# Block scores of the chunked linear attention: seven masks per (head, 128-frame tile) with one multiply and one sum, in place of seven predicated copies per head

## The reference

```
S_t = diag(exp(log_g_t)) S_{t-1} + k_t v_t^T,    o_t = S_t^T q_t
```

## The kernel before

| slot | tile | steps, before |
|---|---|---|
| 18, 20, 21, 22 | f, g, q, v | (2,0)(2,1) / (2,2)(2,3) / (3,0)(3,1) / (3,2)(3,3) |
| 31, 32, 33 | q, v, g | (5,1) / (5,2)(5,3) / (6,0) |
| 35, 36, 37 | g, g, g | (6,1) / (6,2) / (6,3) |
| 38, 39, 40 | none | (7,0) / (7,1) / (7,2)(7,3) |

## Time and profile before

### The profile page before, as it was taken

The page is one execution under the profiler, slowest core; times in us unless marked ns, Lnnn a source line. Parts: engine busy times, 40 slices in busy tenths (PEclk is TensorE's granted clock), DMA queues, the critical chain, the costliest instruction groups (busy, mean ns, idle before and its releaser), DMA issues.

```text
span 1369.5 us, 15843 instructions
## 1 busy us (share of the span) xinstructions
PE 1283.1 (94%) x5841; PEld 1017.8 (74%) x5841; DVE 687.8 (50%) x933; ACT 480.3 (35%) x754; POOL 250.0 (18%) x201
## 2 busy tenths in 40 slices
PE   5899999888889999999997999999799999999996
PEld 3678787676668888888885686656668888888884
DVE  7556767663475343343435555563474343343434
ACT  4444454343233232232433453232333242332322
POOL 2321212201188300000004700000281000000012
PEclk8999999899999999999999999999999999999997
DMA  3321121113214333333332322101223333333321
GB/s 111 108 62 53 41 61 49 46 48 108 77 46 116 93 93 106 94 92 99 95 99 62 77 74 50 46 16 45 78 62 97 100 97 93 97 102 92 92 77 62
DMA packets 212607, 106.62 MB, mean 78 GB/s; under 512 B 20385, under 2 KB 210946, under 8 KB 212546
## 3 DMA queue, kind: packets, MB, share of 16 engines
q1 hardware_dynamic: 211938, 103.42, 26.5%
q0 software_dynamic: 608, 2.36, 0.5%
HBM read 103.67 MB, written 2.10 MB: 77 GB/s over the span
## 4 chain that ended last, share of the span: by engine, by line
PE 84%; DVE 8%; ACT 4%; DMA 2%; issue 1%; POOL 1%; POOLq 0%; ACTq 0%; DVEq 0%; SPq 0%
PE bank L1257 24%; PE bank L1259 24%; PE bank L1258 24%; DVE y L918 2%; PE pp L1372 2%; PE pp L1524 2%; PE pp L1523 2%; PE po L1541 1%; PE pp L1369 1%; DVE h_lo L925 1%; DMA x_tok<-in_x 1%; POOL xT L551 1%; ACT w_hi L403 1%; DVE w_lo L410 1%; PE misc L1303 0%
## 5 line engine op out<-in xcount | busy, mean ns | idle before, releaser
L1257 PE MATMUL bank<-h_lo,w_hi 128*128 128x512 f32 (+1 forms) x848 | 343.9, 406 | 36.7 <-DVE h_lo L925 25.2
L403 ACT CAST w_hi<-stage 128x1024 fp32r<-128x1024 f32 (+2 forms) x192 | 199.1, 1037 | 410.6 <-DMA stage<-in_mlp_w 308.7
L1258 PE MATMUL bank<-h_hi,w_lo 128*128 128x512 f32 (+1 forms) x848 | 335.4, 396 | 0.0
L1259 PE MATMUL bank<-h_hi,w_hi 128*128 128x512 f32 (+1 forms) x848 | 334.7, 395 | 0.0
L410 DVE TENSOR_TENSOR w_lo<-stage,w_hi 128x1024 fp32r<-128x1024 f32 (+2 forms) x192 | 241.6, 1259 | 65.5 <-PE bank L1259 57.2
L1257 PE MATMUL bank<-a_lo,w_hi 128*128 128x512 f32 x656 | 257.1, 392 | 2.2 <-DVE y L1094 2.2
L1258 PE MATMUL bank<-a_hi,w_lo 128*128 128x512 f32 x656 | 255.9, 390 | 0.0
L1259 PE MATMUL bank<-a_hi,w_hi 128*128 128x512 f32 x656 | 255.8, 390 | 0.0
L1257 PEld LDWEIGHTS bank<-h_lo,w_hi 128*128 128x128 f32 (+1 forms) x848 | 161.7, 191 | 86.6 <-issue 41.2
L1258 PEld LDWEIGHTS bank<-h_hi,w_lo 128*128 128x128 f32 (+1 forms) x848 | 161.8, 191 | 35.2 <-issue 2.2
L1259 PEld LDWEIGHTS bank<-h_hi,w_hi 128*128 128x128 f32 (+1 forms) x848 | 161.3, 190 | 35.9 <-issue 0.6
(11 more groups left out here) (244 smaller groups left out, 1149.5 us busy)
## 6 DMA issues: line engine op xcount, KB each, us to landing
stage<-in_mlp_w SPq DMA_DIRECT2D x128, 512.0 KB, 4.1
stage<-in_ev_w_in SPq DMA_DIRECT2D x28, 512.0 KB, 3.7
stage<-in_ev_w_out SPq DMA_DIRECT2D x8, 512.0 KB, 4.1
stage<-in_od_w_out SPq DMA_DIRECT2D x8, 512.0 KB, 4.1
stage<-in_od_w_in SPq DMA_DIRECT2D x5, 512.0 KB, 3.9
x_tok<-in_x SPq DMA_DIRECT2D x4, 512.0 KB, 5.5
x_tok<-in_x POOLq DMA_DIRECT2D x1, 2048.0 KB, 8.4
stage<-in_mla_w_ukv SPq DMA_DIRECT2D x8, 256.0 KB, 3.0
```

The lines of the kernel that those rows point to most:

```text
L403: nc.scalar.copy(w_hi[:, u % SPLIT, 0:n], stage[:, u % STAGE, 0:n]).then_inc(hi_ready, 1)
L1257: nc.tensor.matmul(dst, wh, xl_, start=first, stop=False)
L1258: nc.tensor.matmul(dst, wl, xh, start=False, stop=False)
L1259: return nc.tensor.matmul(dst, wh, xh, start=False, stop=last)
```

## The change

A step becomes one (head, tile) instead of one or two planes for all tiles. PE makes the seven planes of one tile, nine matmuls, into pp0 or pp1 (two of them go round, by p_read). DVE multiplies the 896 columns by the seven masks into tmp and sums the seven planes by a `tensor_reduce` whose innermost axis steps by 128 elements (512 bytes) into one of four 128x128 buffers. Plane 0's mask is now all ones: the parts of plane 0 that no matmul writes are zeroed once at the start (two memsets of 128x128 for one of 128x512). The outputs of a tile follow two long slots behind its own step. The assignment of steps to slots is the same, four per head.

```diff
-            pending = [pending[1], [(o, c) for o, step in groups if step == len(STEPS) - 1 for c in range(NT)]]
+            pending = [pending[1], groups]
@@ pool
-            for r, c in ((slice(0, 64), slice(64, 128)), (slice(0, 32), slice(32, 64)), (slice(64, 96), slice(96, 128))):
-                ch.link(nc.gpsimd.memset(masks[r, 0, c], 1.0))
+            ch.link(nc.gpsimd.memset(masks[:, 0, :], 1.0))
@@ vector
-            nc.vector.memset(pp[0][:, 0:4, :], 0.0).then_inc(p_zero, 1)
+            for b in range(2):
+                nc.vector.memset(pp[b][:, 0, :], 0.0).then_inc(p_zero, 1)
@@
-            def group(o, step):
-                a = a_bufs[o % 2]
-                if step == 0 and o < 2:
-                    nc.vector.memset(a, 0.0).then_inc(a_zero, 1)
-                    dve.wait_ge(a_zero, o + 1)
-                elif step == 0:
-                    dve.wait_ge(o_done, o - 1)
-                for plane in STEPS[step]:
-                    n = o * PAIRS + plane
-                    dve.wait_ge(p_done, n + 1)
-                    if plane:
-                        dve.wait_ge(a_ready, n)
-                    mask = masks[:, plane:plane + 1, :].to_broadcast([P, NT, P])
-                    nc.vector.copy_predicated(a, mask.bitcast(I32), planes[n % 4]).then_inc(a_ready, 1)
-                if step == 2 and FIRST[PACK_OF[o]] == o:
+            def group(o, c):
+                idx = o * NT + c
+                pm = tmp[:, :, :].rearrange("p a t -> p (a t)")[:, 0:PAIRS * P]
+                dve.wait_ge(p_done, idx + 1)
+                if idx >= 1:
+                    dve.wait_ge(a_ready, idx)
+                nc.vector.tensor_tensor(pm, pp[idx % 2][:, 0:PAIRS, :].rearrange("p l t -> p (l t)"),
+                                        masks[:, :, :].rearrange("p l t -> p (l t)"), ALU.mult).then_inc(p_read, 1)
+                dve.wait_ge(p_read, idx + 1)
+                nc.vector.tensor_reduce(a_sb[:, idx % 4, :], pm.rearrange("p (l t) -> p t l", l=PAIRS),
+                                        AX_X, ALU.add).then_inc(a_ready, 1)
+                if c == 2 and FIRST[PACK_OF[o]] == o:
                     update_state(PACK_OF[o])
@@ tensor
-            def pairs(o, step):
...
+            def pairs(o, c):
+                p, idx, r, s = PACK_OF[o], o * NT + c, head_rows(o), slice(c * P, (c + 1) * P)
+                pe.wait_ge(xl_ready, (p + 1) * (LEVELS + 2))
+                if idx >= 2:
+                    pe.wait_ge(p_read, idx - 1)
+                else:
+                    pe.wait_ge(p_zero, idx + 1)
+                for lv in range(2):
+                    L = 64 >> lv
+                    for b in range(0, P, 2 * L):
+                        nc.tensor.matmul(pp[idx % 2][b:b + L, 0, b + L:b + 2 * L], xls[p % 2][r, lv, c * P + b:c * P + b + L],
+                                         xls[p % 2][r, lv, c * P + b + L:c * P + b + 2 * L], start=True, stop=True)
+                for lv in range(2, LEVELS):
+                    nc.tensor.matmul(pp[idx % 2][:, lv - 1, :], xls[p % 2][r, lv, s], xls[p % 2][r, lv, s],
+                                     start=True, stop=True)
+                nc.tensor.matmul(pp[idx % 2][:, PAIRS - 1, :], ks[p % 3][r, s], qs[p % 3][r, s], start=True,
+                                 stop=True).then_inc(p_done, 1)
@@ outputs
-                pe.wait_ge(a_ready, (o + 1) * PAIRS)
-                ins = nc.tensor.matmul(po[:, s], vbuf[:, o % 4, s], a_bufs[o % 2][:, c, :], start=True, stop=(c == 0))
+                pe.wait_ge(a_ready, idx + 1)
+                ins = nc.tensor.matmul(po[:, s], vbuf[:, o % 4, s], a_sb[:, idx % 4, :], start=True, stop=(c == 0))
```

More of the change, by code:

```diff
@@ L46 @@
 PAIRS = 7
-STEPS = [(0, 1), (2, 3), (4, 5), (6,)]
 Q_RANK_T, KV_RANK_T = 3, 2
@@ L297, in trunk @@
         misc = ctx.enter_context(nc.psum_tensor("misc", [P, T], F32))
-        planes = [pp[b][:, h:h + 4, :] for b in range(2) for h in (0, 4)]
-        a_bufs = [a_sb[:, :, :], tmp[:, 0, :].rearrange("p (c t) -> p c t", c=NT)]
         s_bank = [pp[0][:, 0:4, :], pp[0][:, 4:8, :], pp[1][:, 0:4, :]]
@@ L332, in trunk @@
         xl_ready, ket_done, ket_ready = sem("xl_ready"), sem("ket_done"), sem("ket_ready")
-        kv_done, state_ready, p_done, a_zero = sem("kv_done"), sem("state_ready"), sem("p_done"), sem("a_zero")
+        kv_done, state_ready, p_done, p_read = sem("kv_done"), sem("state_ready"), sem("p_done"), sem("p_read")
         a_ready, o_done, o_sq, o_sum = sem("a_ready"), sem("o_done"), sem("o_sq"), sem("o_sum")
@@ L698, in evacuate @@
                 if what in ("q", "k") and i >= 3:
-                    act.wait_ge(p_done, PAIRS * FIRST[i - 2])
+                    act.wait_ge(p_done, NT * FIRST[i - 2])
                 if what == "f":
@@ L970, in decayed @@
                 if lv == 0 and p >= 2:
-                    dve.wait_ge(p_done, PAIRS * FIRST[p - 1])
+                    dve.wait_ge(p_done, NT * FIRST[p - 1])
                 dve.wait_ge(e_ready, done + 2 if lv <= LEVELS else done + 1)
@@ L1349, in head_rows @@
                 return slice(first, first + w_)
-            def pairs(o, step):
[L1352 to L1368, removed]
-                                    ins = nc.tensor.matmul(dst[b:b + L, b + L:b + 2 * L], left, right, start=True, stop=True)
-                        elif plane < PAIRS - 1:
-                            x_ = xls[p % 2][r, plane + 1, s]
-                            ins = nc.tensor.matmul(dst, x_, x_, start=True, stop=True)
-                        else:
-                            ins = nc.tensor.matmul(dst, ks[p % 3][r, s], qs[p % 3][r, s], start=True, stop=True)
-                    ins.then_inc(p_done, 1)
@@ L1377, in outputs @@
             def outputs(o, c):
-                p, r, s = PACK_OF[o], head_rows(o), slice(c * P, (c + 1) * P)
+                p, idx, r, s = PACK_OF[o], o * NT + c, head_rows(o), slice(c * P, (c + 1) * P)
                 if c == 0:
```

## The result

| kernel | median | runs | ratio to before |
|---|---|---|---|
| before | 1370.58 us | 1367.08 to 1372.6 | |
| changed | 1384.22 us | 1383.03 to 1385.23 | 1.0119 [1.0082, 1.0157] |

The medians are those of four runs each, 13.6 us or 1.0% apart. Three further runs of the changed kernel took 1384.99, 1389.55 and 1394.86 us. The ratio rests on all seven: their mean, 1386.6 us, is 16.4 us or 1.2% above the mean of before, 1370.2. One run of e2 (1873.72 us) and one of the kernel before beside it (1871.3 us) had a mean clock of 0.645 and are left out of every figure.

A forecast was written before the change was run, and what follows sets the result against it. PE was taken to set the pace for most of 84 to 311 us, with DVE late in places from slot 31. Terms 0.7 + 0.9 - 1.0 + 1.0 = +1.6 on 1371.2 gave 1372.8 us; range 1368 to 1391.

The forecast's parts named there:

- rival A: The strided sum on DVE runs at half rate, 2.06 us in place of 1.10: 17.6 us slower, 1389 us; chance 0.40.
- The multiply, 1.09 us: DVE's 32 multiplies of 896 columns, PSUM by SBUF, priced between the rows for 512 and 1024 columns.
- The sum, 1.10 us: DVE's 32 sums over 896 elements, priced from dense PSUM reductions at 1.07 ns an element; bounds 0.85 to 2.31.
- Place 4: Slots 35 to 42: clamp, state and gate come later, and DVE has the last head's groups and update; +1.0 us.
- Place 2: Slots 29 to 33: 3.7 us more on DVE against 2.76 idle, so the clamp comes later; +0.9 us.
- Place 3: Slot 33 on PE: first step of head 6 has fewer matmuls, 3.7 us in place of 2.64 + 2.01; -1.0 us.
- Place 1: Slots 20 to 21: the state's update comes later behind two copies' replacement, so head_sum of head 1 waits; +0.7 us.
- Hidden at nothing: Rest of DVE's extra 30 us, slots 12 to 18 and 22 to 28, lies in idle time that a projection ends; 0.
- Rival L: Stated for a follow-up run: only slots 20 and 29 to 42 are costly, so 24 us in slots 12 to 23 cost 0.7 to 3.
- The outputs: Issued one by one, a head's first may wait for o_read of the head before; priced at nothing, upper end 1.6 us.
- A slow stretch goes (B): The slow clock at 160 to 168 us, after slot 21's small matmuls, disappears: 3.2 us faster, 1369.6; chance 0.10.
- Switches of shape (C): On PE each further switch between small and large matmuls costs 0.22 us, 24 times: 5.3 us, 1378; chance 0.07.

The follow-up runs named there:

- e2: Changed kernel with the sum's seven elements read side by side from tmp, so it adds up wrong elements: 1378.96 us, ratio 1.0042.
- e6: Changed kernel with the product written back to PSUM and summed there with its step, PE waiting for the sum: 1377.06 us, ratio 1.0032.
- e9: Kernel before with the first plane of each step copied three times in heads 0 to 3 alone, 23.5 us more on DVE: 1378.39 us, ratio 1.0046.
- e5: Changed kernel with DVE multiplying and densely summing only planes 0 to 3, while PE still makes all seven: 1368.26 us, ratio 0.999.
- e11: Kernel before with steps (0), (1,2), (3,4), (5,6) in place of (0,1), (2,3), (4,5), (6): 1367.01 us, ratio 0.9953.
- e3: Changed kernel with the product written transposed in steps of 28 bytes, so that the sum reads densely: 1390.42 us, ratio 1.0129.
- e7: Kernel before with planes 0 to 5 copied only over the right halves, 256 or 384 columns for 512: 1372.19 us, ratio 1.0005.

## Why the prediction was right or wrong

The time lies in the range because the range was stretched to take in rival A. The forecast had +1.6 us where +13.6 was measured (+16.4 in the mean of seven runs), and its own range, 1369 to 1377, was missed.

- **The multiply, 1.09 us:** right (1.084), as was the two operations' place in the order.
- **The sum, 1.10 us:** the step that failed. "I take 1.10, since the row of the same operation is the nearest." It measured 1.763, inside its bounds (0.85 to 2.31). What decides is how far apart the elements lie in SBUF, and no row of the trace of before has such a step. The prediction saw this as A's mechanism and took the other value. A was right in kind; its size, 2.06, was an upper case: 1.76 is 1.6 times the dense duration, not twice. The rule of "SBUF — State Buffer" in the Trainium skill (section "Door 1: The DMA port swizzle"), at least two hits in each 16-byte line, fits the sums: 8 bytes, two elements to a line, cost nothing (1086 ns), and 16 bytes cost nearly all (1721). The same passage of the Trainium skill has 4 fp32 as the free reach of a stride; read as a step, that is 16 bytes, and the measured sum doesn't bear it out. "VectorE: DVE Perf Modes" in the Trainium skill (section "The perf-mode tier table"), with one element a cycle from any memory, fits the dense sums (1085 from SBUF, 1091 from PSUM) and not this one.
- **Place 4:** +7.2, close to A's 6.6, against 1.0. With a dense sum it is +2.5 and +3.1, so it was short there too.
- **Place 2:** +3.5. With a dense sum +1.1 and +1.4, right against 0.9.
- **Place 3:** -0.9, right, by the lighter first step of head 6.
- **Place 1:** +4.9 (+4.6 from 84.78 on), but not by the mechanism. head_sum of head 1 starts at 165.57 with no wait, since PE is still at the projection when the state stands at 162.45. Some 3.4 of it are clock: in stretches of 4 us the changed kernel loses 6.8 us of full speed between 84 and 184, before 3.4. In e2 the clock takes 5.1 of 6.4, in e6 6.8 of 7.8. Without it 1.0 to 1.3 are left in all three, near the 0.7 of the forecast and far from A's 7. (A's own terms give 17.8 - 7.2 - 2 to 3, which is 8, not 7.)
- **Hidden at nothing:** e9 puts 16 of its 23.5 us ahead of the state in slot 20, more than the idle time there, and the excess comes out as the wait of head_sum for the state that the prediction had priced as place 1, and in rival A at 7 us for 17.8. So the rule "hidden until it has used up that idle time" held. Rival L is a narrower map than the prediction's, and what e9 refutes is that 24 us more in these slots cost at most 3. Whether the forecast's own 0.71 us a step was hidden there, only e2 and e6 show: +0.9 and -0.7 between places 1 and 2.
- **The outputs:** priced at nothing, with a wait for o_read as the danger. There was none. They waited for the state (4.3 us) and the sums (4.0) instead, in slots 36 to 42; the forecast had expected the wait for the state at head_sum, where none is left.
- **A slow stretch goes (B):** it didn't, it came earlier and lasted longer. In the changed kernel, against 0.70 and 0.50 in the earlier trace rows:

```profile
152.00:156.00 4.00, 4.00 (x29) 3.49 (x26) 3.63 (x7) 3.63 (x9) 0.84 (x1) 0.50 0.47 135
156.00:160.00 4.00, 4.00 (x11) 3.10 (x11) 3.97 (x6) 1.09 (x2) 1.47 (x2) 0.50 0.00 0
160.00:164.00 4.00, 4.00 (x15) 3.14 (x15) 3.90 (x6) 0.00 (x0) 0.00 (x0) 0.76 0.00 0
```

- **Switches of shape (C):** in slot 16 a tile's nine matmuls take 0.10 us longer than the same in long rows, an estimated 3.2 us for all in place of 5.3. It should have been a term of the sum, not a rival; how much of it reaches the kernel's time is not shown alone (e5: ratio 0.999, +2.0 us at equal clock).
- **With the right sum:** putting 1.09 us in gives the forecast's own kernel, e2 or e6. By the ratios it measured +5.8 and +4.4 (intervals 1.9 to 9.6 and 1.8 to 6.9) against +1.6. So the sum's duration accounts for 10 to 12 of the 15 us that were missing by the ratios, and for 8 of 12.5 at equal clock. The rest fits the order on PE (2.0 in e5) and place 4 (1.5 and 2.1 above the forecast with a dense sum), but no run takes these two apart.

What stays open: why the clock falls in one run of the same rows and not in another. Where e2 falls to 0.50 at 116 to 120 us, e5 stays at 1.00 with the same matmuls in the same order. Whether the gain of e11 would hold in a kernel changed elsewhere was not tried.

## What to carry to other kernels

Price an operation by how its operands lie in memory before its name: the row of the same operation with dense reads is no price for one whose elements lie 16 bytes or more apart, and where no row has the pattern, the bound from the mechanism deserves the larger chance. Keep such intermediates in PSUM (e6): a dense read that is bought with a stepped write costs as much again (e3), and e2's dense read adds up the wrong elements. And idle time in front of an engine covers work only until its sum over a run of slots is used up; it is safer to add the extra up slot by slot against the idle time than to call a stretch covered.

## What the runs showed of the hardware that was not expected

- VectorE, 896 fp32 elements: a sum takes 1085 ns dense or at 8 bytes, 1721 at 16, 1753 at 32, 1658 at 512 in SBUF, and 1091 from PSUM at 512 bytes; an add with two reads at 512 bytes 2016, a multiply that writes at 28 bytes 1756.
- A predicated copy of 256 elements takes 0.43 us in runs of 4 or more, and 0.73 in runs of two every 16 bytes or single ones every 8 (e7).
- The same instructions (e5) take 1364.28 us in a run at a mean clock of 0.976 and 1376.67 in one at 0.967. In e11 a change of the order on TensorE goes with a mean of 0.9732 against 0.9687, some 4.7 us by the slope, with hardly any other gain.
